# A four-layer hybrid decoder trunk on 8 cores: layer 0's weights cast again for every tile, a staging buffer moved, small loads on another queue

## The reference, cut to what matters

```python
h = layer_norm(x) * (1 + scale) + shift          # shift, scale, gate = silu(c) @ w_c + b_c  (the "modulation")
u = h @ w_in                                      # eight 1024-wide projections
xa = causal_conv4(a_x) + b;  r, i = sigmoid(blockdiag gates of xa)
a = exp(-8 r softplus(-lam));  hs = scan(a, sqrt(1 - a*a) * i * xa)      # h_t = a_t h_(t-1) + b_t
o_a = (hs * silu(a_z)) @ w_a_out
o_b = (b_bg * causal_conv3(b_cg * b_x) * silu(b_z)) @ w_b_out
out = (sigmoid(g_a) * o_a + sigmoid(g_b) * o_b) @ w_o
x = layer_norm(ALPHA * x + gate * out) * ln_g + ln_b
```

## Time and profile before

| | |
|---|---|
| median of 3 runs | 3167.64 us |
| the profiled execution | 3174.04 us |
| span of its slowest core (core 1), the one shown | 3171.7 us |
| spans of all cores | 3133.4 to 3171.7 us |
| busy, share of the span | PE 90%, DVE 65%, ACT 62%, POOL 33% |
| chain that ended last | PE 70%, DMA 9%, ACT 7%, DVE 6%, issue 6% |
| cast loads | 228 (176 + 48 + 4), 512 KB each as written |
| scratch writes, scratch reads | 180, 532 of 512 KB |

### The profile page before, as it was taken

One profiled execution on the slowest core, in us unless ns is written; L12 is line 12 of the kernel. 1 busy time (PEld: TensorE's weight loads), 2 busy tenths in 40 slices (PEclk: granted clock), 3 DMA queues, 4 the chain that ended last, 5 costly groups with the idle time before them and its releaser, 6 DMA issues.

```text
span 3171.7 us, 57032 instructions; the slowest of 8 cores (3133.4 to 3171.7 us)
## 1 busy us (share of the span) xinstructions
PE 2868.1 (90%) x16224; PEld 1390.6 (44%) x16224; DVE 2058.8 (65%) x3583; ACT 1981.1 (62%) x3257; POOL 1057.9 (33%) x1626
## 2 busy tenths in 40 slices
PE   3778899899988999989999899999999989998996
PEld 2344444344444444444445444444444434443443
DVE  3565576676757767577674776668655865667564
ACT  3566564777647767377754776558664866558651
POOL 1334331454314443144330333215321442225222
PEclk9989999999999999999999999999999999999998
DMA  7999756989659897398674445434444334433442
GB/s 155 213 230 207 171 168 145 227 199 218 163 131 226 210 221 191 104 221 218 192 187 133 158 163 173 140 127 140 142 145 132 120 127 154 139 127 127 146 154 99
DMA packets 144723, 526.91 MB, mean 166 GB/s; under 512 B 16057, under 2 KB 16185, under 8 KB 144418
## 3 DMA queue, kind: packets, MB, share of 16 engines
q1 hardware_dynamic: 111586, 403.72, 38.0%
q0 software_dynamic: 32832, 119.55, 24.2%
HBM read 538.05 MB, written 104.69 MB: 203 GB/s over the span
## 4 chain that ended last, share of the span: by engine, by line
PE 70%; DMA 9%; ACT 7%; DVE 6%; issue 6%; POOL 2%; SPq 0%; POOLq 0%; DVEq 0%; ACTq 0%
PE PS L536 65%; DMA WB<-wmain 4%; DMA WB<-scr 3%; PE PS L790 2%; PE PS L793 2%; ACT L500 2%; DVE PXA L522 1%; PE PS L543 1%; DMA LT<-xp 1%; ACT PXA L500 1%; DVE X L515 1%; POOL PTI L515 1%; DMA WB<-wc 1%; DMA LT<-cvec 1%; DVE PTR L917 1%
## 5 line engine op out<-in xcount | busy, mean ns | idle before, releaser
L536 PE MATMUL PS<-HN,WB 128*128 128x512 bf16 (+1 forms) x10240 | 1963.0, 347 | 105.7 <-DMA WB<-wmain 24.4
L536 PEld LDWEIGHTS PS<-HN,WB 128*128 128x128 bf16 x10240 | 865.0, 99 | 1100.9 <-issue 208.0
L500 ACT ACT_TABLE_LOAD x285 | 365.7, 1283 | 116.0 <-PE PS L536 50.7
L522 DVE SCALAR_TENSOR_TENSOR PXA<-PAX,PRM,PXA 128x512 f32<-128x512 f32 x384 | 317.0, 827 | 98.3 <-ACT PXA L500 83.6
L522 DVE SCALAR_TENSOR_TENSOR PTAB<-PTAB,PS 128x512 f32<-128x512 f32 x256 | 174.2, 684 | 234.7 <-PE PS L536 178.8
L500 ACT ACTIVATE PTAB<-PS 128x512 f32<-128x512 f32 x256 | 151.0, 595 | 205.9 <-PE PS L536 184.1
L500 ACT ACTIVATE LNR<-X 128x512 fp32r<-128x512 f32 (+1 forms) x272 | 139.7, 535 | 197.2 <-PE PS L793 145.0
L536 PE MATMUL PS<-YA,WB 128*128 128x512 bf16 (+1 forms) x1280 | 256.6, 344 | 2.7 <-issue 1.7
L536 PE MATMUL PS<-YB,WB 128*128 128x512 bf16 (+1 forms) x1280 | 254.4, 342 | 5.0 <-DVE STAB L522 2.3
L536 PE MATMUL PS<-MG,WB 128*128 128x512 bf16 (+1 forms) x1280 | 241.7, 348 | 12.8 <-DVE MG L515 10.9
L515 POOL TENSOR_TENSOR YA<-PTR,PTZ 128x512 bf16<-128x512 f32 x128 | 182.6, 1427 | 197.7 <-DVE PTR L917 190.0
(11 more groups left out here) (145 smaller groups left out, 3664.5 us busy)
## 6 DMA issues: line engine op xcount, KB each, us to landing
WB<-scr SPq DMA_DIRECT2D x528, 512.0 KB, 4.1
WB<-wmain POOLq DMA_DIRECT2D x176, 512.0 KB, 11.8
scr<-WB SPq DMA_DIRECT2D x176, 512.0 KB, 10.4
WB<-wc POOLq DMA_DIRECT2D x48, 512.0 KB, 10.3
LT<-xp SPq DMA_DIRECT2D x28, 512.0 KB, 5.9
yp<-LT SPq DMA_DIRECT2D x8, 512.0 KB
X<-xp SPq DMA_DIRECT2D x4, 512.0 KB, 15.7
WG<-wmain POOLq DMA_DIRECT2D x4, 512.0 KB, 11.6
```

The source lines that it names most:

```text
L500: return P.add("act", lambda e: e.activation(out=out, in_=in_, func=func, **kw), reads, writes, cost=cost, lat=0.17, tbl=TBL.get(func, 0))
L522: return ew("dve", lambda e: e.scalar_tensor_tensor(out=out, in0=in0, scalar=scalar, in1=in1, op0=op0, op1=op1), out, [in0, in1], reads, w ...
L536: ins = e.matmul(out, l_, r_, start=(i == 0), stop=(i == n - 1))
```

## The change

Five things, all in the order and the kind of loads; what is computed does not change.

1. Layer 0's 45 units (u < UNITS_PER_LAYER) are cast loads for every tile. Their 45 scratch writes are gone, and 133 scratch reads (44 for tile 1, 45 for tile 2 with the gates, 44 for tile 3) become cast loads. Layers 1 to 3 keep the scratch.
2. Tile 0's rows are staged in phase 1's own buffers (the rings TR, TI, A, TBZ, 1024 columns each), one 4 KB piece per row, and no cast load waits for them any more. X(1) moves from the end of phase 1 to the end of phase 2.
3. The identity, the conditioning vectors (`cvec`) and the parameters (`prm`) are issued by ACT, no longer by SP.
4. Layer 0's own units 8 to 11 of the modulation go one group later.
5. The next layer's 12 modulation units, all in phase 2 before, are spread: eight in phase 2, four in phase 3.

```diff
-                       4: [("HE", 1, 1), ("LN0",)], 5: [("M", 0, 8), ("M", 0, 9)],
-                       6: [("X", 1), ("M", 0, 10), ("M", 0, 11)]}
+                       4: [("HE", 1, 1), ("LN0",)], 6: [("M", 0, 8), ("M", 0, 9)],
+                       7: [("M", 0, 10), ("M", 0, 11)]}
...
-                for i in range(6):
-                    ex2[i] = [("M", l + 1, 2 * i), ("M", l + 1, 2 * i + 1)]
+                for i in range(4):
+                    ex2[i + 1] = [("M", l + 1, 2 * i), ("M", l + 1, 2 * i + 1)]
             if l == 0:
                 ex2[5] = ex2.get(5, []) + [("X", ta)]
+                if ta == 0:
+                    ex2[7] = [("X", 1)]
...
+                if not last:
+                    ex3[2] = [("M", l + 1, 8), ("M", l + 1, 9)]
+                    ex3[5] = [("M", l + 1, 10), ("M", l + 1, 11)]
...
-    early = [XB[c][1] for c in range(NCH)]
...
-        if t is None or t == 0:
+        if t is None or t == 0 or u < UNITS_PER_LAYER:
             srcd = wc_d[u] if t is None else wmain_d[u]
...
-            if t == 0:
+            if t == 0 and u >= UNITS_PER_LAYER:
...
-            load_unit(WB[slot], WBB[slot], slot, *seq[j], reads=early if 2 <= j < 10 else [])
+            load_unit(WB[slot], WBB[slot], slot, *seq[j])
...
             if t == 0:
-                sl = X[:, 2 * tb:2 * tb + 2, 512:1024]
-                sB = [XB[2 * tb][1], XB[2 * tb + 1][1]]
+                r = RP[("TR", "TI", "A", "TBZ")[tb], "p"]
+                sl = r.t[:, :].rearrange("p (a b) -> p a b", b=512)
+                sB = r.b
...
-        P.add("sp", lambda e: e.dma_start(out=IDN[:, :], in_=ident_d), writes=[IDNB], dma="misc", cost=0.1, lat=2.2)
+        P.add("act", lambda e: e.dma_start(out=IDN[:, :], in_=ident_d), writes=[IDNB], dma="misc", cost=0.1, lat=2.2)
...
-        P.add("sp", lambda e: e.dma_start(out=io[:17, :], in_=cvec_d), writes=iob, dma=f"io{k}", cost=0.1, lat=2.2)
-        pst, bb = rows_T(prm_d, 64)
+        P.add("act", lambda e: e.dma_start(out=io[:17, :], in_=cvec_d), writes=iob, dma="cv", cost=0.1, lat=2.2)
+        pst, bb = rows_T(prm_d, 64, "act")
```

More of the change, by code:

```diff
@@ L546, in v3, with rows_T @@
         return ap.rearrange("p (b t) -> p b t", t=inner)
-    def rows_T(src_ap, nrows):
+    def rows_T(src_ap, nrows, eng="sp"):
         k, io, iob = next_io()
-        P.add("sp", lambda e: e.dma_start(out=io[:nrows, :], in_=src_ap), writes=iob, dma=f"io{k}", cost=0.1, lat=2.2,
+        P.add(eng, lambda e: e.dma_start(out=io[:nrows, :], in_=src_ap), writes=iob, dma=f"io{k}{eng}", cost=0.1, lat=2.2,
               xfer=1.6)
```

## The result

| | before | after |
|---|---|---|
| median | 3166.07 us (4 runs) | 3126.97 us (4 runs) |
| the profiled execution | 3174.04 us | 3124.62 us |
| spans of the cores | 3133.4 to 3171.7 us | 3096.9 to 3123.1 us |
| casts, scratch writes, scratch reads | 228, 180, 532 | 361, 135, 399 |

The ratio is 0.9877, with a 95% interval of 0.9854 to 0.9899: 39 us or 1.2% faster, inside what the forecast called "within 2%", where 58 us had been worked out.

A forecast was written before the change was run, and what follows sets the result against it. DMA was taken to bound layer 0's phase 1 and start of phase 2 in the first pair, partly the rest of phase 2. Terms -71 + 4 - 3 + 12 = -58 us gave a median forecast of 3110 us, range 3076 to 3146.

The forecast's parts named there:

- within 2%: Whole kernel: a time within about 2% (63 us) of before, indistinguishable from no change; chance 0.54.
- -71 + 4 - 3 + 12: Whole kernel: layer 0 up to P3, its phase 3, modulation in layers 1 and 2, second pair's layer 0; -58 us.
- P3 of tile 0 in the changed kernel: Layer 0, first pair: first P3 at 343 us instead of 414, bounds 328 and 363.
- the step that priced a `cvec` landing at 26 us at nothing: Start: even with cvec landing at 26 us, nine casts keep DMA busy to about 40 us.
- 71 us earlier: Layer 0, first pair: first P3 comes 71 us earlier than the 414 us of before, bounds 51 and 86.
- phase 3 of layer 0, +4: Phase 3 of layer 0: thin DMA cover and PE time of four modulation units cost 4 us (0 to 10).
- modulation, -3: Layers 1 and 2: four fewer modulation units in each phase 2, their matmuls in phase 3; gain 3 us (0 to 8).
- layer 0 of the second pair, +12: Second pair's layer 0: 89 scratch reads become casts on POOL; cost 12 us (0 to 25).
- Rival 4: Second pair's layer 0: POOL's casts and the copies behind them form a loop holding PE; 3254 us, chance 0.06.
- rival 1: Layer 0: PE's chain bounds it, or cvec is late; P3 only 51 us earlier, 3130 us, chance 0.21.
- Rival 2: Layer 0: all casts hidden, bound 328 us reached, second pair loses nothing; 3081 us, chance 0.15.
- Rival 3: POOL: casts held at issue, 133 more at 0.27 us each give 36 us back; 3146 us, chance 0.05.

The follow-up runs named there:

- cvec16: The changed kernel with the load of cvec's 17 rows cut into one of 16 rows and one of 1 row; ratio 0.9864 to the kernel before.
- spread_only: The kernel before with only the next layer's modulation units spread, eight in phase 2 and four in phase 3; ratio 0.9866 to the kernel before.
- m_back: The changed kernel with modulation units back where they were, all twelve of the next layer in phase 2; ratio 0.9957 to the kernel before.
- m_shift: The changed kernel with all twelve modulation units of the next layer in phase 2, groups 1 to 6, none in phase 3; one time, 3129.9 us.
- cast_only: The kernel before with only layer 0's units cast for all four tiles and their scratch writes gone; ratio 0.9923 to the kernel before.

## Why the prediction was right or wrong

**Within 2% held, the sum did not.** 58 us were worked out and 39 measured. In the order of the sum, -71 + 4 - 3 + 12, the marks give -56 + 20 - 10 + 8: two terms were 31 us too good together, two 11 us too bad. That the result still lay in the range is in part the luck of errors that offset each other.

**Right: P3 of tile 0 in the changed kernel.** Worked out 343 us, measured 346. Within it errors cancelled: the first projection at 57 and not 52, then 133 us to first BA (bounds 112 to 129) and 156 to P3 (bounds 169 to 176), both outside. The late first projection comes from the step that priced a `cvec` landing at 26 us at nothing: it landed at 25, and with the vectors there 10 us earlier (`cvec16`) the first projection comes at 48. That DMA is what fills the time up to P3 holds: 0.99, 0.92 and 0.98.

**Wrong in its base: 71 us earlier.** On the profiled core 1 it was 67 (413 to 346). But that core was among the last: the median core had its first P3 at 402, and two at 390. Over the cores the term is 56. I allowed for the profiled execution lying 6.4 us above the median, and not for its slowest core being late in the very stretch that the change shortens. Profile to profile the change gives 49 us, medians to median 39.

**Wrong in its parts: who earns it.** I named the scratch writes as the cause. The 56 us are 28 for the casts, 18 for four modulation casts fewer ahead of P3 (14 by 4 x 3.47), 10 for the other three edits (forecast for the start: 16). One stall in it I had read but not named: in the kernel before, SP holds its own queue for scratch writes that wait for their casts, and the row loads of tile 1 stand behind them. SP's waits of core 0 from 40 to 410 us, and PE's of core 1 from 68 to 238 us, in the kernel before:

```profile
SPq L209 <- DMA WB<-wmain: 192.2, 35, 28.9
```

```profile
PE PS L543 <- ACT LT L500: 19.1, 1, 19.1
```

The load that took 26.8 us in the earlier trace rows was issued at 133 us behind such a write, and PE waited 19 us for its transposes. In the changed kernel SP waits for no cast into WB up to 410 us, and the wait of PE's transposes for ACT's LT is 0.2 us. How much of the 28 us this stall is, no run separates.

**Wrong: phase 3 of layer 0, +4, measured +20.** "Its cover is thin, no longer half empty" was right, the price was not. DMA's sum does fit (0.72 x 144 = 104 us, I had 109), but buffers come free in bursts. The parts, each from the run that undid it or did it alone: modulation units 10 to 14 us, X(1) 4, casts 2 to 4. The move of X(1) I had not priced at all.

**Wrong: modulation, -3, measured -24 in layers 1 to 3 when alone.** I read 1 us per cast off two phases 2. But phase 1 before it runs at DMA 0.96 too: the eight casts taken out of the two stretches shorten them by 30 us, 3.47 x 8 = 28 by the price, and lengthen phases 3 by 18. `spread_only` and `m_back` agree on the size (24 and 30 us in layers 1 to 3), though both times lay outside the ranges that I had given; `m_shift` puts some 12 of the 30 on group 0 left free, which is no price of a cast. That layer 3, which holds no modulation, also gets 12 us shorter (398 to 386) is not explained by this.

**Too high: layer 0 of the second pair, +12, measured +6** (360 to 366 us), PE 133 of 136 us at DMA 0.89. Rival 4 falls: no loop of casts and copies.

**Missing: a term for what comes after.** With the casts, layers 1 to 3 took 14 us more, once without the spread (1224 against 1210) and once with it (1200 against 1186). The first of these is the less sure: taken core by core and then the median, it is 8 (1220 against 1212), the second still 14. Nothing in those layers was changed by edit 1, so the sum had no term for it. In the measured sum -56 + 20 - 10 + 8 = -38 the -10 is -24 for the spread and +14 for this.

**The rivals.** The result lies 3 us from rival 1's 3130, but not by its mechanism: PE was no bound (P3 at 346, not 363); its clause on a late `cvec` did come true. Rival 2 falls with phase 3. Rival 3 falls too: the casts did not get dearer. DMA's own queue for casts in the changed kernel, 57 to 190, 190 to 346 and 1698 to 2064 us (packets, MB, share):

```profile
q0 software_dynamic: 4805, 17.48, 84.8%
...
q0 software_dynamic: 6302, 22.96, 92.1%
...
q0 software_dynamic: 11929, 43.42, 70.2%
```

33.3 casts in 0.848 x 133 us, 43.8 in 0.921 x 156, 82.8 in 0.702 x 366: 3.38, 3.28 and 3.10 us each, where 3.47 was the price before. The Trainium skill (SBUF — State Buffer, "SBUF: two separate sides") says that such loads starve while VectorE runs an operation that uses both ports. Casts beside a DVE busy 75% of the first of these stretches show no such price; how much of that time was such operations is not read from the trace.

**Open.** What costs the 8 to 14 us in layers 1 to 3 and, with the spread, 10 in the second pair; and what the spread gains in layer 3. The scheduler orders the whole program anew for every variant: in the traces the sequence of TensorE's work in `cast_only` differs from that before in all layers of the first pair. Whether the order or the later state of the buffers takes the head start was not tried, and singles of under 10 us above may be such an order too.

## What to carry to other kernels

Price a transfer by the whole stretch that waits for DMA, up to the next point where DMA is idle, and not by the phase it stands in, and charge the place where it goes: in layers 1 and 2 eight casts, moved out of stretches at 0.96 into phases at 0.46, took 30 us off the one and put 18 on the other. Take the base of a term from the median core of the trace, not from the slowest. And a head start early in a program is no gain until a later mark shows it: beside the spread the casts brought P3 28 us forward and the end by 2; alone they brought the end 12 forward by the marks.

## What the runs showed of the hardware

A load of 17 rows and 68 KB, issued at 2.3 us beside nine casts, took 23.0 us; 16 of its rows, 64 KB, issued at 1.7 us, took 7.1 to 8.8 us. Its own queue alone did not help it: from SP's queue it had taken 20.9 us. A cast of 512 KB took 3.1 to 3.4 us of all DMA engines in the changed kernel, 3.45 to 3.48 in the kernel before, with scratch traffic beside it and with next to nothing beside it; no run shows what makes the difference.
